# A tenth slot of expert weights, and gate rows sent through a small table in main memory

## What is computed

```python
mod_l = (s_c @ ada_w[i] + ada_b[i])[:, None, :]
sh1_l, sc1_l, g1_l, sh2_l, sc2_l, g2_l = jnp.split(mod_l, 6, axis=-1)
...
x_l = x_l + g1_l * out_l
...
    x_l = x_l + g2_l * swiglu(f_l, ev_ffn_wg[j], ev_ffn_wu[j], ev_ffn_wd[j])
...
    x_l = x_l + g2_l * moe_swiglu(f_l, od_router[j], od_exp_wg[j], od_exp_wu[j], od_exp_wd[j])
```

## Times and profile before

| | |
|---|---|
| Three runs | 1997.56, 1997.46, 1995.81 us; median 1997.46 |
| The profiled execution | 1995.97 us, its span 1994.1 us |
| TensorE busy | 1845.4 us, 93% of the span |
| VectorE, ScalarE, GpSimd busy | 665.8, 491.0 and 426.6 us |
| Moved by DMA | 482.24 MB, 242 GB/s over the span |
| Granted TensorE clock, mean | 0.974 of full |

### The profile page before, as it was taken

One profiled execution on the slowest core, in us unless ns is written; L12 is line 12 of the kernel. 1 busy time (PEld: TensorE's weight loads), 2 busy tenths in 40 slices (PEclk: granted clock), 3 DMA queues, 4 the chain that ended last, 5 costly groups with the idle time before them and its releaser, 6 DMA issues.

```text
span 1994.1 us, 23074 instructions
## 1 busy us (share of the span) xinstructions
PE 1845.4 (93%) x9645; PEld 1105.0 (55%) x9646; DVE 665.8 (33%) x1201; ACT 491.0 (25%) x814; POOL 426.6 (21%) x240
## 2 busy tenths in 40 slices
PE   4999988999999979989979899999999999987996
PEld 2777457977777758878745443333433334332432
DVE  4964765644000033470163342111321013211222
ACT  3333345633222112342253211011011011111111
POOL 1432654541333333444541000000000000000000
PEclk8999999999999989989989999999999999999998
DMA  9354000225454442137215799999989998999996
GB/s 355 113 188 181 1 1 1 72 99 170 165 174 169 169 169 84 64 100 170 91 31 225 319 414 410 401 388 395 396 338 388 412 390 317 411 411 412 412 413 258
DMA packets 149868, 482.24 MB, mean 242 GB/s; under 512 B 26388, under 2 KB 51397, under 8 KB 135413
## 3 DMA queue, kind: packets, MB, share of 16 engines
q1 hardware_dynamic: 149296, 479.85, 63.1%
q10 hardware_dynamic: 453, 0.65, 0.1%
HBM read 479.43 MB, written 1.05 MB: 241 GB/s over the span
## 4 chain that ended last, share of the span: by engine, by line
PE 66%; DVE 4%; SPq 4%; DMA 3%; issue 1%; ACT 1%; POOL 1%; DVEq 0%; ACTq 0%
PE PS L2704 21%; PE PS L2721 11%; PE PS L2132 8%; PE PS L2133 8%; PE PS L2134 8%; SPq L641 3%; PE PS L2665 2%; PE PS L2675 1%; DMA BIG<-in_od_exp_wu 1%; PE PS L2620 1%; PE PS L2695 1%; DMA BIG<-in_od_exp_wg 1%; PE PS L2111 1%; SPq L638 1%; DVE X L1728 1%
## 5 line engine op out<-in xcount | busy, mean ns | idle before, releaser
L2704 PE MATMUL PS<-BIG,QB 128*64 128x448 f32 x1424 | 303.4, 552 | 21.0 <-DMA BIG<-in_od_exp_wu 11.6
L2721 PE MATMUL PS<-BIG,ZS 128*64 128x512 f32 x966 | 218.0, 593 | 2.7 <-ACT ZS L1309 2.7
L2704 PEld LDWEIGHTS PS<-BIG,QB 128*64 128x64 f32 x1424 | 109.4, 140 | 191.9 <-issue 190.4
L703 POOL TENSOR_TENSOR BIG_parts<-BIG,QB_parts 128x2048 fp32r<-128x2048 f32 x33 | 152.8, 4631 | 267.2 <-ACT QB_parts L880 267.2
L2704 PE MATMUL PS<-BIG,HB 128*64 128x448 f32 x944 | 200.2, 546 | 10.2 <-issue 9.2
L703 POOL TENSOR_TENSOR BIG_parts<-BIG,BIG_parts 128x2048 fp32r<-128x2048 f32 (+1 forms) x26 | 119.1, 4582 | 201.0 <-ACT BIG_parts L880 201.0
L2721 PEld LDWEIGHTS PS<-BIG,ZS 128*64 128x64 f32 x966 | 70.7, 137 | 135.2 <-issue 134.3
L2133 PE MATMUL PS<-HB_parts,QB_parts 128*128 128x512 f32 (+1 forms) x384 | 143.5, 374 | 0.0
L2704 PEld LDWEIGHTS PS<-BIG,HB 128*64 128x64 f32 x944 | 72.2, 138 | 122.0 <-issue 120.8
L1309 ACT ACTIVATE ZS<-PS 128x896 f32<-128x896 f32 x32 | 29.4, 918 | 418.9 <-PE PS L2695 418.9
L2051 DVE TENSOR_TENSOR MOD<-QB,PS 64x448 f32<-64x448 f32 x32 | 19.7, 615 | 267.0 <-ACT QB L1303 257.1
(11 more groups left out here) (400 smaller groups left out, 3085.3 us busy)
## 6 DMA issues: line engine op xcount, KB each, us to landing
BIG<-in_od_exp_wg SPq DMA_DIRECT2D x63, 1792.0 KB, 17.8
BIG<-in_od_exp_wu SPq DMA_DIRECT2D x56, 1792.0 KB, 14.0
BIG<-in_od_exp_wd SPq DMA_DIRECT2D x55, 1792.0 KB, 18.2
BIG<-in_ada_w SPq DMA_DIRECT2D x24, 2048.0 KB, 8.6
QB<-in_od_exp_wd SPq DMA_DIRECT2D x9, 1792.0 KB, 13.8
QB<-in_od_exp_wu SPq DMA_DIRECT2D x8, 1792.0 KB, 14.7
BIG<-in_od_w_qkv SPq DMA_DIRECT2D x6, 2048.0 KB, 11.4
BIG<-in_ev_ffn_wg SPq DMA_DIRECT2D x11, 1024.0 KB, 8.7
```

What stands on the lines that cost most here:

```text
L703: pool.tensor_tensor(r12(w), w, r12(high), ALU.subtract).then_inc(split_l, 1)
L2704: last = mm(PS[at:at + 64, bank, 0:GROUP], XGS[x][:, 4 * part + k, r0:r0 + 64], wgu[u][:, k, GROUP * c:GROUP * c + GROUP], start=(part + k ...
L2721: last = mm(PS[64 * n:64 * n + 64, bank, :], HET[:, s % 2, k, r0:r0 + 64], half[:, a, :], start=(k == 0), stop=(k == 6))
```

## The change

Two things, which hang together by the space they use.

1. `SLOTS_E` goes from 9 to 10. The new slot 9 is the tile `XT` (free since early in the program). Its arrivals are counted on the semaphore `outside_arrived`, which counted the one chunk that `XT` held before. Expert 7 still uses eight slots.
2. No gate row goes through TensorE. `store_gates` writes the rows from `MOD` to a table in main memory (`GROWS`, 32 KB), and `load_gate` reads a row back into all 128 partitions by one DMA with a step of 0. All are issued by SP, at four places: rows for out0 before `w_out` is loaded; rows for the feed-forward before chunk `up3`; layer 1's store before the first qkv chunk; and layer 1's two rows at the start of natt, ahead of the rpb windows of pairs 12 to 15. Twelve products on TensorE go, and the copies out of PSUM on DVE and ACT (four on DVE, eight on ACT). `GB0` moves to `XT`, gate 1 of layer 1 to a free part of `HB`.

```diff
-        GB0 = AR[:, 0:2 * D].rearrange("p (r n) -> p r n", r=2)
+        GB0 = XT[:, 0:2 * D].rearrange("p (r n) -> p r n", r=2)
+        GA1 = HB[:, 2048:2048 + D]
...
+        GROWS = nc.dram_tensor("gate_rows", (2, 2, 2, D), f32, kind="Internal").ap()
...
-        arrived_e = [sem(f"expert_weights_arrived{i}") for i in range(RING_E + 1)]
+        arrived_e = [sem(f"expert_weights_arrived{i}") for i in range(RING_E + 1)] + [arrived[RING]]
...
-        SLOTS_E = RING_E + 1
+        SLOTS_E = RING_E + 2
...
-            return arrived_e[at], 16 * n, expert_slot(at)
+            before = 16 * loads_before[RING] if at == RING_E + 1 else 0
+            return arrived_e[at], before + 16 * n, expert_slot(at)
...
+            if at == RING_E + 1:
+                return XT[:, 0:SLOT_E]
...
+            def store_gates(l, n):
+
+                sp.wait_ge(mod_rows, 3 * l + 3)
+                for which in range(2):
+                    for c in range(2):
+                        q = 32 * (2 * which + c)
+                        sp.dma_start(GROWS[l, which, 0:n, 512 * c:512 * c + 512],
+                                     MOD[q:q + n, 1 + which, :]).then_inc(gates_in, 16)
+
+            def load_gate(to, l, which, r):
+
+                row = bass.AP(tensor=GROWS.tensor, offset=((2 * l + which) * 2 + r) * D, ap=[[0, P], [1, D]])
+                sp.dma_start(to, row).then_inc(gates_in, 16)
...
+                if i == first["out0"]:
+                    store_gates(0, 2)
+                    sp.wait_ge(tok_mm, 8)
+                    sp.wait_ge(gates_in, 64)
+                    for r in range(2):
+                        load_gate(GB0[:, r, :], 0, 0, r)
+                if i == first["up3"]:
+                    sp.wait_ge(out_mm, 2 * NT)
+                    for r in range(2):
+                        load_gate(GB[:, r, :], 0, 1, r)
+                if i == first["qkv"]:
+                    store_gates(1, 1)
...
+            begin(sp, None, "natt")
+            sp.wait_ge(gates_in, 192)
+            load_gate(GA1, 1, 0, 0)
+            load_gate(GE, 1, 1, 0)
...
-            dve.wait_ge(gb_mm, 1)
             dve.wait_ge(go_sum, NT)
-            for r in range(2):
-                for c in range(2):
-                    last = dve.tensor_copy(GB0[:, r, 512 * c:512 * c + 512], PS[:, 4 + 2 * r + c, :])
-            last.then_inc(gb_ready, 1)
...
-                dve.wait_ge(gb_ready, 1 if stage == "out0" else 4)
+                dve.wait_ge(gates_in, 96 if stage == "out0" else 224)
...
             begin(pe, "pe", "gout")
-            gate_rows(1, 0, 2)
...
-            for r, c, bank in FFN_GATES[0:3]:
-                last = gate_row(2, 2, r, c, bank)
-            last.then_inc(gb_mm, 1)
...
-                if f == 2:
-                    pe.wait_ge(gb_ready, 2)
-                    gate_row(2, 2, *FFN_GATES[3]).then_inc(gb_mm, 1)
...
             begin(pe, "pe", "out1")
-            gate_rows(1, 0, 1)
-            gate_rows(2, 2, 1, 6)
```

More of the change, by code:

```diff
@@ L478, in build @@
         sm_tr, sm_cols = sem("small_transposed"), sem("small_columns")
-        mod_rows, ada_tr, gb_mm = sem("mod_rows"), sem("ada_transposed"), sem("gate_rows_mm")
+        mod_rows, ada_tr, gates_in = sem("mod_rows"), sem("ada_transposed"), sem("gates_in")
         norm_sd, norm_rstd, xn_ready, norm_tr, norm_ev = (sem(n) for n in (
@@ L516, in pair @@
             return 4 * s + 2 * d + i + 1
-        gb_ready, go_tr, go_ev, go_sd, go_n = (sem(n) for n in ("gate_rows_ready", "o_transposed", "o_columns", "o_sd",
+        go_tr, go_ev, go_sd, go_n = (sem(n) for n in ("o_transposed", "o_columns", "o_sd",
                                                                 "o_gated"))
@@ L1130, in _ @@
             act.nop().then_inc(done["act"], 1)
[L1132 to L1136, removed]
-                    for c in range(2):
-                        last = act.activation(to[:, r, 512 * c:512 * c + 512], PS[:, 4 + 2 * r + c, :], ACT.Copy)
-                last.then_inc(gb_ready, 1)
-                act.wait_ge(gb_ready, k + 1)
             begin(act, "act", "out0")
@@ L1174, in _ @@
                 act.nop().then_inc(done["act"], 1)
[L1176 to L1181, removed]
             for f in range(FF // P):
@@ L1260, in _ @@
             attention(N_PAIRS, NM, PC, PCT, 2, DH ** -0.5)
-            gate_rows("out1", 3, GB, 1)
-            act.wait_ge(gb_mm, 5)
-            for c in range(2):
-                last = act.activation(GE[:, 512 * c:512 * c + 512], PS[:, 6 + c, :], ACT.Copy)
-            last.then_inc(gb_ready, 1)
+            begin(act, "act", "out1")
             act.activation(SS[:, 20:21], EPSC[:, 0:1], ACT.Sqrt)
@@ L1725, in add_out @@
                     dve.wait_ge(out_mm, base + i + 1)
-                    gate, tmp = (GB0[:, t // 2, cols], OT) if stage == "out0" else (GB[:, t // 2, cols], ZS)
+                    gate, tmp = (GB0[:, t // 2, cols], OT) if stage == "out0" else (GA1[:, cols], ZS)
                     seq(dve.tensor_tensor(tmp[:, i % 2, :], PS[:, i % 4, :], gate, ALU.mult))
@@ L1808, in roots_2 @@
                 dve.reciprocal(SS[:, 16 + 2 * h:18 + 2 * h], SS[:, 8 + 2 * h:10 + 2 * h]).then_inc(norm_rstd, 1)
+            dve.wait_ge(gates_in, 128)
             for t in range(NT):
@@ L2455, in _ @@
             end()
-            def gate_row(g, c0, r, c, bank):
-                q = 32 * (c0 + c) + r
-                return mm(PS[:, bank, :], ident()[:, q:q + 1].to_broadcast([P, P]), MOD[:, g, :], start=True, stop=True)
-            def gate_rows(g, c0, n, bank=4):
-                for r in range(n):
-                    for c in range(2):
-                        last = gate_row(g, c0, r, c, bank + 2 * r + c)
-                last.then_inc(gb_mm, 1)
             begin(pe, "pe", "gout")
-            gate_rows(1, 0, 2)
             def mixed_parts(k, cols):
@@ L2487, in _ @@
                 first_half(1, t)
-            pe.wait_ge(gb_ready, 1)
             for t in range(NT):
```

9 lines of the change are left out of this document (removed).

## The result

| | before | after |
|---|---|---|
| Median of four runs | 1997.51 us (1995.81 to 1997.78) | 1982.05 us (1981.28 to 1983.33) |
| The profiled execution | 1995.97 us, span 1994.1 us | 1981.28 us, span 1979.5 us |
| TensorE busy | 1845.4 us | 1830.5 us |
| Moved by DMA | 482.24 MB | 485.42 MB |

The ratio is 0.9925 with a 95% interval of 0.9908 to 0.9942: 15.0 us faster (11.6 to 18.4). The forecast was 1985.0 us in a range of 1980.5 to 1991.5. The profiled execution is 14.7 us shorter, where the sum said 12.3.

The account below looks back on a forecast made before the run. TensorE was taken to bound the experts until 1681 us, then DMA without pause; 8.5 + 3.6 + 2.8 - 2.6 = 12.3 us off gave 1985 us against the runs' median, range 1980.5 to 1991.5.

Parts of the forecast that it names:

- the sum: Whole kernel: the gains 8.5, 3.6 and 2.8 us less the loss of 2.6 us, 12.3 us faster in all.
- The experts' end, with the rows of out1: Experts' weights and start of out1: tenth slot and four removed gate products together gain 8.5 us, bounds 3.7 to 9.7.
- The up stage: Up stage: gate products leave TensorE's chain, gaining 3.6 us; the replacing loads cost nothing, or up to 2.6 us if uncovered.
- gout: gout: 3.67 us of products go, but DVE's multiplications then limit the turns, so 2.8 us remain, bounds 0 and 3.7.
- natt: Start of natt: two row loads ahead of the windows of pairs 12 to 15 lose 2.6 us, bounds nothing and 6.6.
- The lower bound: Start of natt: the row loads cost nothing if they fit in gaps the windows' small packets leave.
- Few DMA engines: Row loads in natt: each confined to one engine, windows up to 41.6 us late, 26.7 us slower, 2024 us; chance 0.04.
- Later windows: natt: loads cost 6.6 us and gout gives only 1, leaving 6.5 us gained, 1991 us; chance 0.14.
- The slot does nothing: Experts' end: the tenth slot gives nothing, the end moves by PE's 3.7 us only, 7.5 us in all, 1990 us; chance 0.08.
- Everything goes well: Whole kernel: 9.7 + 3.6 + 3.7 - 0 = 17.0 us gained, 1980.5 us; chance 0.08.
- The parts cancel: natt: a delay of 10 to 18 us cancels the gains, leaving the time within 0.2%; chance 0.04.

Follow-up runs that it names:

- the four rows: The changed kernel with two more 512 KB row loads, content unused, ahead of layer 1's two at natt's start: 1984.92 us, ratio 0.9938 to the kernel before.
- the first experiments: For the figure given, the changed kernel run again as it is, against the kernel before on the same chip: 1984.11 us, ratio 0.9934.

## Why the prediction was right

The time came out 3 us below the forecast of 1985.0, inside the range, and the difference of the two profiled executions is 14.7 us where the sum said 12.3. Point by point:

- **The experts' end, with the rows of out1: predicted 8.5 us, measured 8.2** (from natt's end, where the changed trace is 6.5 us ahead, to the last down product, where it is 14.7). The start of out1 in the chain of waits, after, beside 1063.34 in the earlier trace rows:

```profile
1056.84 27.72 PE PS L2602 x64
```

  The counting of chunks through the rounds was right: 127 goes with the earlier release, 128 waits, and the pause is no shorter. (Before, the slots of chunks 116 and 117 were refilled one behind the other, at 1660.71 and 1661.12; the prediction names only the first time for 117, which changes nothing in the step.) Stretch G gives 4.5 for the slot, and the products 3.7. The step through landing times came out a little high because the gaps between two landings, 4.3 to 5.2 us, aren't what a slot is worth in the end; one chunk at DMA's rate, 4.5 us, is.
- **The up stage: predicted 3.6, measured 3.4**, and 3.5 when the products came back. The cover held. ACT does wait longer for a weight, but no row of the list of waits has PE waiting for it. Waits in the up stage, after, beside the earlier trace rows:

```profile
ACT QB_parts L916 <- DMA BIG<-in_ev_ffn_wu: 7.7, 5, 4.3
```

  That is 5.5 us more on ACT in all, 3.2 more at worst, for 2.6 us of DMA put in front.
- **gout: predicted 2.8, measured 2.2 up to the turns, and 3.6 for the stretch.** The limit behind the products was the right one (DVE's multiplications, started by ACT's root). The rest of the deviation is DVE's 4.70 us where the row had 4.29, and PE's last quarter, 0.66 us and not 0.48. The 1.4 us beyond are the clock in out0, which the prediction had nowhere. It compared the stages' work at one clock.
- **natt: predicted a loss of 2.6 us, measured 0.6** to natt's end in this pair of traces, 0.8 with out1's first products, and 1.2 as a mean over the traces: D without the products' 3.67 us is 80.4 and 79.8 in the two traces of kernels that have no rows in natt, and 81.3 in the mean of the six with two rows and no products (80.95 to 81.48). This is the step that failed: "I take the full 2.6 us as a loss". The price of the rows was right: the first window lands 2.6 us later. But the mask waits for the last of four windows, which goes out 2 us after the first and lands only 1.7 us later, and of that 1.2 us reach out1. So about half of the term was never paid. That the time between the issues covers it is my reading. The lower bound named another cover, "gaps that the windows' small packets leave", and the four rows speak against that one.
- The sum was thus short by 2.0 us in natt and 0.8 in gout and out0, and long by 0.3 at the end and 0.2 in the up stage: 2.3 of the 2.4 us between 12.3 and 14.7. The start (0.3 shorter) and C (0.2 longer), which the change hardly touches, make up the rest.
- Two parts of this are luck. The 1.4 us of clock in out0 are no merit of the sum, and the pair of traces that was compared has natt 0.4 us better than the mean (a loss of 0.8 up to out1's first products, for 1.2). On the chip of the first experiments the changed kernel is 14.3 us faster by the medians, with a ratio of 0.9934 instead of 0.9925.

The rivals. **Few DMA engines**: the rows in natt went by at a share of 0.98 and 352 GB/s, and POOL waited 1.17 us more (1.7 as a mean), not 41.6; it falls. **Later windows**: natt's loss stayed under 2.6 us; even twice the rows cost 3.1 us more and not another 6.6; it falls. **The slot does nothing**: without it G is 4.5 us longer; it falls. **Everything goes well** (1980.5 us) came nearer to the measured 1982.05 than the forecast of 1985 did, for other reasons than it gave: its 9.7 us at the release were 8.2, and gout and out0 gave 3.6 of its 3.7 only with the help of the clock. In natt, where it put nothing, this pair of traces lost 0.6 us. **The parts cancel**: nothing of it.

## What to carry to other kernels

A prefetch slot that is added to a ring whose end is bound by DMA is worth one chunk at DMA's rate. It doesn't shorten the pause of the queue (19.95 us with eight, nine and ten slots), it moves it one chunk further; and it is worth that once, at the last forced pause, as long as the part before it is bound by TensorE and never waits. Where it does wait, as with eight slots, the slot is worth more. A broadcast made on TensorE costs its own time if the chain runs through it, and a broadcasting load of the same row costs nothing where the queue has slack. Where it is put in front of small transfers that are issued one by one, part of its DMA time may not be paid (here half of 2.6 us), and all of it is for what comes on top.

## What the runs showed that I had not expected

**The clock, and work that stands ahead of a gap.** Without the products in gout, a stall of TensorE in out0 comes 2.2 us earlier with its length unchanged, and a fall of the granted clock worth 1.4 us is gone, in all nine traces of such kernels. A difference of that size that no instruction accounts for is to be looked for in the clock first.

**DVE beside GpSimd.** What TensorE waits for in out0 is one addition on DVE. In the changed kernel's timeline:

```profile
420.11 0.69 DVE L1733 TENSOR_TENSOR X<-X,BIG 128x512 f32<-128x512 f32 x1
...
421.25 4.56 POOL L739 TENSOR_TENSOR BIG_parts<-BIG,BIG_parts 128x2048 fp32r<-128x2048 f32 x1 [6.97 <-ACT BIG_parts L916]
421.44 4.92 DVE L1733 TENSOR_TENSOR X<-X,BIG 128x512 f32<-128x512 f32 x1
```

The same addition takes 0.69 us alone and 4.92 us when GpSimd's subtraction of 4.56 us has started 0.2 us before: it ends 0.6 us after that one. DVE's other operation there, which reads one of its inputs from PSUM, keeps its 0.69 us beside GpSimd's next one, and again the addition behind it does not:

```profile
436.89 4.61 POOL L739 TENSOR_TENSOR BIG_parts<-BIG,QB_parts 128x2048 fp32r<-128x2048 f32 x1 [1.60 <-ACT QB_parts L916]
437.62 0.69 DVE L1732 TENSOR_TENSOR BIG<-PS,XT 128x512 f32<-128x512 f32 x1 [8.61 <-PE PS L2140]
438.34 3.70 DVE L1733 TENSOR_TENSOR X<-X,BIG 128x512 f32<-128x512 f32 x1
```

The addition of 4.92 us is in the kernel before too and no part of this change; moving the two apart wasn't tried.
